# mLSTM with tokens on the partitions, its preparation in the input product, and the later modulation panels in the attention

## The reference

```python
h = rms_norm(x, norm_mix[l])
z = h @ w_in[l]
(m_q, m_k, m_v, m_o, m_i, m_f, a_q, a_k, a_v, i_q, i_k, i_w) = split_cols(z, IN_SIZES)
qk = silu(causal_dwconv(concat([m_q, m_k]), mlstm_conv_w[l], mlstm_conv_b[l]))   # 4 taps
hm = mlstm_chunkwise(q, k, m_v, m_i + i_bias[l], m_f + f_bias[l])                # 4 heads, 64 / 128 wide
hm = sigmoid(m_o) * rms_norm(hm, mlstm_norm[l])
ha = dsa_attention(a_q, a_k, a_v, i_q, rms_norm(i_k, idx_k_norm[l]), i_w * IDX_HEADS ** -0.5, rel_bias)
x = x + concat([hm, ha]) @ w_out[l]
```

## Time and profile before

| | |
|---|---|
| median of 3 runs | 3762.57 us (3760.34 to 3766.36) |
| the profiled execution | 3759.47 us, span 3757.6 us |
| PE busy | 3365.8 us, 90% |
| DVE busy | 1935.9 us, 52% |
| ACT busy | 1489.5 us, 40% |
| POOL busy | 562.7 us, 15% |
| `in1`, until the last gate tile is taken | about 213 us |
| mLSTM stage | 213.6 to 336.9 us |
| index stage and `rel` block | 336.9 to 443.7 us |
| attention stage | 443.7 to 549.2 us |

### The profile page before, as it was taken

The page is one execution under the profiler, slowest core; times in us unless marked ns, Lnnn a source line. Parts: engine busy times, 40 slices in busy tenths (PEclk is TensorE's granted clock), DMA queues, the critical chain, the costliest instruction groups (busy, mean ns, idle before and its releaser), DMA issues. The chain is left out here.

```text
span 3757.6 us, 38218 instructions
## 1 busy us (share of the span) xinstructions
PE 3365.8 (90%) x13472; PEld 2359.3 (63%) x13472; DVE 1935.9 (52%) x2317; ACT 1489.5 (40%) x1918; POOL 562.7 (15%) x304
## 2 busy tenths in 40 slices
PE   7976699999899979597999897799999999999976
PEld 6742465887545558465888544577676777777752
DVE  2046533334424450425003324788888888888835
ACT  3223123443234433113223101566666666565623
POOL 3400002444100024212445100000000000000010
PEclk9966659999999989799999997899999999999988
DMA  3220501222121112121222611899999999999940
GB/s 135 107 90 34 190 1 67 93 108 90 68 83 52 67 45 90 67 90 45 93 108 90 271 67 70 361 398 401 400 401 398 402 404 396 406 395 405 396 191 23
DMA packets 69955, 713.67 MB, mean 190 GB/s; under 512 B 7408, under 2 KB 7792, under 8 KB 29424
## 3 DMA queue, kind: packets, MB, share of 16 engines
q1 hardware_dynamic: 58704, 670.10, 45.1%
q0 software_dynamic: 7056, 25.69, 1.7%
q10 hardware_dynamic: 4112, 16.78, 1.1%
HBM read 672.17 MB, written 40.37 MB: 190 GB/s over the span
## 5 line engine op out<-in xcount | busy, mean ns | idle before, releaser
L136 POOL TENSOR_TENSOR ring_low<-ring,ff_ring_high 128x1024 fp32r<-128x1024 f32 x136 | 331.5, 2471 | 924.0 <-ACT ff_ring_high L131 924.0
L197 PE MATMUL psum<-ff_high,ff_ring_high 128*128 128x512 f32 x832 | 326.0, 392 | 23.2 <-DVE h_low L337 8.6
L199 PE MATMUL psum<-ff_high,ring_low 128*128 128x512 f32 x832 | 325.3, 391 | 0.0
L197 PE MATMUL psum<-ex_high,ex_rows_high 128*128 128x512 f32 x768 | 316.3, 412 | 6.8 <-DVE ring_low L2359 6.8
L199 PE MATMUL psum<-ex_high,ex_rows_low 128*128 128x512 f32 x768 | 301.8, 393 | 0.0
L198 PE MATMUL psum<-h_low,ff_ring_high 128*128 128x512 f32 x704 | 275.1, 391 | 0.0
L2359 DVE TENSOR_TENSOR ex_more_low<-ex_more,ex_high_in_x 128x2048 fp32r<-128x2048 f32 x96 | 219.5, 2286 | 70.4 <-ACT ex_high_in_x L2286 70.4
L2359 DVE TENSOR_TENSOR ring_low<-ring,ex_high 128x2048 fp32r<-128x2048 f32 x96 | 214.3, 2287 | 40.3 <-ACT ex_high L2286 40.3
L1338 PE MATMUL psum<-h,ring 128*128 128x512 f32 x512 | 224.0, 594 | 1.1 <-ACTq L1409 1.1
L2248 PE MATMUL psum<-ex_more,ex_act_t 128*128 128x512 f32 x512 | 224.9, 592 | 0.0
L2286 ACT ACTIVATE ex_high<-ex_more 128x1024 fp32r<-128x1024 f32 x192 | 200.5, 1062 | 57.4 <-PE psum L199 57.4
(11 more groups left out here) (508 smaller groups left out, 6703.7 us busy)
## 6 DMA issues: line engine op xcount, KB each, us to landing
ex_more<-moe_w SPq DMA_DIRECT2D x128, 2048.0 KB, 9.7
ring<-wstream SPq DMA_DIRECT2D x87, 2048.0 KB, 8.1
ring<-moe_w SPq DMA_DIRECT2D x64, 2048.0 KB, 12.0
ex_bias_up<-moe_b SPq DMA_DIRECT2D x32, 1024.0 KB, 8.5
y_rows<-ex_y SPq DMA_DIRECT2D x33, 512.0 KB, 9.2
y_rows<-mx_zero ACTq DMA_DIRECT2D x1, 16384.0 KB, 51.8
ex_bias_down<-moe_b SPq DMA_DIRECT2D x32, 512.0 KB, 8.4
x<-xt SPq DMA_DIRECT2D x8, 256.0 KB, 5.7
```

Of the source, the lines that this page charges most:

```text
L136: e.tensor_tensor(low, full, high.bitcast(F32), ALU.subtract).then_inc(self.low_ready, 1)
L197: pe.matmul(out, a[0], b[0], start=start, stop=False)
L199: return pe.matmul(out, a[1], b[0], start=False, stop=stop)
```

## The change

- **Input product.** The panel with `ik` and the gates comes fourth instead of last. `i`, `f` and `iw` are one tile of 72 rows (i on rows 0 to 3, f from 32, iw from 64) instead of six tiles; `iw` is transposed in the mLSTM stage. The convolution, the Silu of `qk`, the Silu of the modulation's condition and the gates' rows are done in this stage, between the takes (`Rows.act_step`, `Rows.dve_step`, `Rows.convolve`).
- **mLSTM.** Tokens lie on the partitions. The triangular mask is a minimum with 0 or -1e30 before the exponential, on the four diagonal squares alone; the exponential of the rest reads the spread maximum straight from PSUM with the key's value as bias. Numerator and denominator are one product of 129 columns (`mv` has a column of ones, set by POOL). Denominator, floor, norm and root are then 128 x 4 for a head; ACT scales the numerator, PE transposes it, and DVE multiplies by the norm's weight and the gate. Buffers of `prob` and banks alternate by head, and the next head's spread, limits and exponentials are issued ahead.
- **Modulation.** `EARLY = 4`: four products in the mLSTM stage, columns of these in the index stage behind the index scores, the other eight products in the attention at n = 2, 5, ... 23 in bank 7, with their rows copied by ACT, and their 32 columns at n = 32.
- **`rel`** is loaded by SP at the start of the index stage and waited for by DVE at the attention's start; its own block goes. `turn_heads` uses bank 6 alone.

The diff, cut to its core:

```diff
@@ class Modulation
-    EARLY = 3
+    EARLY = 4
@@ class Rows (new)
+    def act_step(self, act, i, tile_ready, dve_took, bank):
+        if i == 7: ... cond = Silu(c2)
+        if i < 4:
+            act.wait_ge(tile_ready, i + 1)
+            act.activation(b1["iq"][:, i, :], bank, ACT.Identity, scale=col("conv_w", 3 * 4 + i),
+                           bias=col("conv_b", i)).then_inc(self.based, 1)
+        if 4 <= i < 8:
+            act.wait_ge(dve_took, i - 3)
+            act.activation(b1["qk"][:, i - 4, :], b1["iq"][:, i - 4, :], ACT.Silu).then_inc(self.qk_ready, 1)
...
+    def convolve(self, dve, i, bank):
+        dve.wait_ge(self.based, i + 1)
+        for tap in (2, 1, 0):
+            back = M_CONV - 1 - tap
...
+            to = b1["iq"][:, i, back:]
+            done = dve.scalar_tensor_tensor(to, bank[:, 0:S - back], col("conv_w", tap * 4 + i), to, ALU.mult, ALU.add)
@@ mlstm_stage, ScalarE
+                def weights(h):
+                    b = h % 2
+                    act.wait_ge(limited, TT * (h + 1))
+                    for j in ORDER:
+                        part = prob[:, b, AT[j]:AT[j] + P]
+                        act.activation(part, part, ACT.Exp).then_inc(weighted, 1)
+                        if j < TT - 1:
+                            act.activation(prob[:, b, AT[j] + P:AT[j] + S - P * j], max_bank[:, P * (j + 1):S], ACT.Exp,
+                                           bias=a_col[:, j, h:h + 1]).then_inc(weighted, 1)
...
+                    if h == 0:
+                        weights(1)
+                        for p in range(2, 4):
+                            act.wait_ge(panel_done, 4 * (p + 1))
+                            mo.take(act, p, psum[:, 4 + p, :]).then_inc(row_ready, 1)
+                    elif h + 1 < MH:
+                        weights(h + 1)
+                    for i in range(TT):
+                        act.wait_ge(nd_done, TT * h + 2 * (i // 2) + 2)
...
+                        act.activation(junk[:, i % 2, :], num(h, i)[:, 0:M_DV], ACT.Square,
+                                       accum_out=squares[:, TT * h + i:TT * h + i + 1]).then_inc(squared, 1)
+                    act.wait_ge(den_ready, 4 * h + 4)
+                    act.activation(den[:, at], den[:, at], ACT.Sqrt).then_inc(std_ready, 1)
+                    act.wait_ge(inverted, h + 1)
...
+                        act.activation(scaled_num[:, q, i, :], num(h, i)[:, 0:M_DV], ACT.Copy,
+                                       scale=inv[:, TT * h + i:TT * h + i + 1]).then_inc(scaled, 1)
@@ mlstm_stage, TensorE
+                for h in range(MH):
+                    if h + 1 < MH:
+                        spread_of(h + 1)
+                    if h == 0:
+                        pe.wait_ge(row_ready, 2)
+                    if h == 1:
+                        pe.wait_ge(row_ready, 4)
+                    if h:
+                        turn(h - 1)
+                    if h >= 2:
+                        pe.wait_ge(mixed, h - 1)
+                    products(h)
+                    if h + 1 < MH:
+                        scores_of(h + 1)
+                    if h == 0:
+                        pe.wait_ge(floor_ready, 1)
+                        for p in range(2, 4):
+                            mo.product(g, pe, p, psum[:, 4 + p, :], panel_done, p + 1)
+                turn(MH - 1)
@@ index_stage
-                for p in range(mo.EARLY, N_ADA):
...
-                    mo.product(g, pe, p, psum[:, p % 4, :], panel_done, done)
+                mo.columns(g, pe, psum[:, 4, :], 0, mo.EARLY).then_inc(columns_ready, 1)
...
-                ring.load_until(sp, FIRST["w_ada"] + N_ADA + SLOTS)
+                sp.dma_start(rel[:, :, :], g.rel_bias).then_inc(rel_in, 16)
@@ attention_stage
+        panel_at = {2 + EVERY * (p - mo.EARLY): p for p in range(mo.EARLY, N_ADA)}     # EVERY = 3
...
+                    if n in panel_at:
+                        done = panel_at[n] - mo.EARLY
+                        if done:
+                            pe.wait_ge(row_ready, done)
+                        mo.product(g, pe, panel_at[n], row_bank, panel_done, done + 1)
+                    if n == NI:
+                        pe.wait_ge(row_ready, N_ADA - mo.EARLY)
+                        mo.columns(g, pe, row_bank, mo.EARLY, N_ADA).then_inc(columns_ready, 1)
...
+                dve.wait_ge(rel_in, 16)
                 soft(0)
```

More of the change, by code:

```diff
@@ L410, in dense_stage @@
                         lambda e, t: e.wait_ge(dve_took, t + 1))
+        if rows is not None:
+            rows.open(sem)
         taken = {"act": [], "dve": []}
@@ L512, in _ @@
                         t.take(dve, psum[:, i % BANKS, :]).then_inc(dve_took, 1)
+                    if rows is not None:
+                        rows.dve_step(dve, i)
                     if sums is not None:
@@ L768, in take, with columns, add_bias @@
         return act.activation(self.part(p), bank, ACT.Copy)
-def mlstm_stage(g, b1, mix, mo):
+    def columns(self, g, pe, bank, first, end):
+        for j in range(4 * first, 4 * end):
+            mm = pe.matmul(bank[:, j:j + 1], self.part(j // 4, j % 4 * P, P), g.ones[:, 0:1], start=True, stop=True)
+        return mm
+    def add_bias(self, g, dve, bank, first, end):
+        at, part = COLS.at["b_ada"], slice(4 * first, 4 * end)
+        return dve.tensor_tensor(g.mod[:, part], bank[:, part], g.cols[:, at + 4 * first:at + 4 * end], ALU.add)
@@ L820, in _ @@
-                for t in range(4):
-                    act.wait_ge(conv_done, t + 1)
-                    act.activation(b1["qk"][:, t, :], conv[:, t, :], ACT.Silu).then_inc(qk_ready, 1)
-                for p in range(mo.EARLY):
+                def weights(h):
[7 more added lines that the diff above has]
+                                           bias=a_col[:, j, h:h + 1]).then_inc(weighted, 1)
@@ L848, in _, with spread_of @@
             @block.tensor
             def _(pe):
-                pe.wait_ge(cond_ready, 2)
-                for p in range(mo.EARLY):
-                    mo.product(g, pe, p, psum[:, 1 + p, :], panel_done, p + 1)
-                pe.wait_ge(rows_ready, 2)
+                def spread_of(h):
+                    if h:
+                        pe.wait_ge(weighted, 7 * h)
+                    pe.matmul(max_bank, g.neg_head[:, h, :], rows.max_row[:, :], start=True, stop=True).then_inc(spread, 1)
@@ new lines, in products, with turn @@
+                def products(h):
+                    for i in range(TT):
+                        pe.wait_ge(prob_ready, 3 * h + min(i, 2) + 1)
+                        for j in range(i + 1):
+                            at = AT[j] + (i - j) * P
+                            mm = pe.matmul(num(h, i), prob[:, h % 2, at:at + P], b1["mv"][:, j, h, :], start=j == 0, stop=j == i)
+                        mm.then_inc(nd_done, 1)
+                def turn(h):
+                    pe.wait_ge(scaled, TT * (h + 1))
+                    for i in range(TT):
+                        mm = pe.transpose(turn_bank(h)[:, i * P:(i + 1) * P], scaled_num[:, h % 2, i, :], g.ident)
+                    mm.then_inc(turned, 1)
@@ new lines, in _ @@
+                spread_of(0)
+                for j in range(TT):
+                    mm = pe.matmul(psum[:, 6, MH * j:MH * j + MH], rows.m_row[:, j * P:(j + 1) * P], g.ident[0:MH, 0:MH],
+                                   start=True, stop=True)
+                mm.then_inc(mcol_psum, 1)
+                for j in range(TT):
+                    mm = pe.matmul(psum[:, 5, IH * j:IH * j + IH], b1["raw"][64:64 + IH, j * P:(j + 1) * P],
+                                   g.ident[64:64 + IH, 64:64 + IH], start=True, stop=True)
@@ L1232, in block_1 @@
             for m in range(4):
-                to = b1[name][:, m, :]
                 e = "act" if m % 2 or name == "o_gate" else "dve"
-                take = copy[e](to) if name != "o_gate" else \
-                    (lambda to: lambda a, bank: a.activation(to, bank, ACT.Sigmoid))(to)
-                tiles.append(Tile([n0 + p], 0 if tokens else m * P, PANEL if tokens else P, h, to, e, take,
-                                  tokens=m if tokens else None, halves=(high, g.h_low)))
-        last = [n0 + 7]
@@ L1265, in block_1 @@
+        mlstm_stage(g, b1, rows, h, mo)
+        with nc.sbuf_tensor("mask", [P, TT, S], F32) as mask, nc.sbuf_tensor("rel", [P, AH, S], F32) as rel:
+            rel_in = g.kept.enter_context(nc.semaphore("rel_in"))
+            index_stage(g, b1, mask, mo, rel, rel_in)
+            attention_stage(g, b1, mask, rel, rel_in, h, mo)
     with ExitStack() as own:
```

415 lines of the change are left out of this document (220 added, 195 removed).

## The result

The changed kernel takes 3645.64 us (median, 3643.75 to 3650.99) against 3761.45 us (3760.01 to 3766.36) for the kernel before in the same comparison: a ratio of 0.9692, interval 0.9675 to 0.9709, or 3.1% faster. The profiled execution has a span of 3641.9 us at a mean granted clock of 0.944 (before: 3757.6 us, 0.926).

What follows compares the result with a forecast made beforehand. TensorE was 90% busy, partly at reduced clock, with limits taken stage by stage: PE, an engine-to-engine chain in mLSTM, DVE in the index stage. Terms -18.1 - 58 - 28.3 + 34.4 = -70 from 3759.5 gave 3690 us, range 3664 to 3714.

Steps and rivals of the forecast that it cites:

- Part 1: Input product: six tiles become one, less a 3.6 us stall waiting for the next panel; -18.1 us.
- Part 3: Index stage: attention starts 0.6 us after the search instead of 28.9, `rel` and early columns hidden; -28.3 us.
- rival D: Attention: panel transfers stand open and products wait for them, slower than before at 3770 us; chance 0.01.
- Part 4: Attention: eight products and 32 columns added, 6 us given back by the clock; +34.4 us, bounds +20 and +43.
- rival A: Attention goes to full clock and stays there, 3648 us; chance 0.10.
- Part 2: mLSTM stage: shorter, overlapping heads of 8.3 to 12 us, length 65 us (bounds 55 and 77); -58 us.
- B: mLSTM and attention: PE-bound at half clock with no gift from the clock, 3707 us; chance 0.22.
- C: mLSTM: DVE or ACT bound by small steps, handoffs costing 26 us more, 3716 us; chance 0.05.

Runs made afterwards that it cites:

- e7_late_burst: Kernel before plus one unused burst of 16 dense matmuls at head 23 of the attention: 3745.12 us, ratio 0.9958.
- e10_mid_burst: Kernel before plus one unused burst of 16 dense matmuls at head 15 of the attention: 3734.74 us, ratio 0.9932.
- e1_burst: Kernel before plus one unused burst of 16 dense matmuls at head 2 of the attention, turn_heads using bank 6 alone: 3762.67 us, ratio 1.0008.
- e2_bursts: Kernel before plus eight unused bursts of 16 dense matmuls, at attention heads 2, 5, ... 23, turn_heads using bank 6 alone: 3743.25 us, ratio 0.9959.
- e11_columns26: Changed kernel with the later columns in one stretch at head 26 instead of behind the last head: 3652.03 us, ratio 0.9716.
- e6_early2: Changed kernel with modulation panels 2 and 3 also moved from the mLSTM into the attention: 3640.54 us, ratio 0.969.
- e8_head0: e4_columns with the eight later products at heads 0, 3, ... 21 instead of 2, 5, ... 23: 3657.73 us, ratio 0.9724.
- e4_columns: Changed kernel with the 32 later columns made panel by panel at heads 4, 7, ... 25 instead of all at head 32: 3637.14 us, ratio 0.9679.
- e9_all: combo with the later products at heads 0, 3, ... 27: 3631.74 us, ratio 0.966.
- combo: Changed kernel with the edits of e6_early2 and e4_columns together: 3635.65 us, ratio 0.9674.

## Why the prediction missed

**The sign and half the steps** held. Part 1 came out at -18.2 for -18.1, with the stall at the place, by the engine and to the time that were worked out. Part 3 came out at -28.4 for -28.3, `rel` and the early columns hidden as costed, and no transfer ever released a product of the attention (rival D's condition).

**Part 4, the give-back of the clock,** is the step that failed. I took 6 us for "where it rises, the next few us of the attention run up to twice as fast" and gave 0.10 to rival A, whose mechanism is what happened for 68 of the stage's 100 us (341.4 to 409.7). Measured against its terms: eight products 17.1 us (one of 3.64, seven of 1.92) where the sum had 27.3 and A had 15.3; the column passes 13.8 us, as the sum had them (13.4), since the clock had fallen by then; all else in the stage 100.4 - 17.1 - 13.8 = 69.5 us for 105.5, so 36 us less where the sum had some 6 and A had 29. Together -5.1 for +34.4. That A's time, 3648, lies so near the measured one is partly luck: its columns were 7 us too cheap and its heads 7 us too dear, and it had the mLSTM 9 us too long and nothing given back. My evidence against A was that 105 us at 96% busy had never risen. That showed that the heads do not raise the clock; e7_late_burst and e10_mid_burst show that the long ones keep it once it is up, two different questions that I took for one. The row that spoke for A, the full clock at a light load from 355 to 360, was weighed too low. The sentence of the Trainium skill, "TensorE: Matmul & The Clock Gate", section "What's actually happening", that I set against the earlier trace rows ("activity releases the throttle") is borne out by the runs of added bursts, as far as dense matmuls go (e1_burst, e7_late_burst, e10_mid_burst; the first burst of e2_bursts raised nothing); the heads' own activity did not release it, and one-column matmuls ended it (e11_columns26).

**Part 2, the length of the mLSTM,** had the right mechanism and too large a size: 65 us taken, 56.8 measured. I took the scores at half clock from the stage before the change, where PE stood between long holes. With fewer holes they ran at 2.42 us from head 1 on, and e6_early2 shows that this needs no panels 2 and 3. That the stage ended at 251.9, where full clock throughout had been worked out to end at 251, is partly luck, since the clock was 0.80 in the mean and the products of heads 1 and 2 ran largely at half. Head 0 waited for modulation row 3 as listed, and the head periods of 9.0 to 6.5 us begin within 8.3 to 12 and end below, the last ones having no next head's weights on ScalarE.

**Rivals.** B and C would have been slower than the forecast and did not show (ScalarE waited 0.25 us for VectorE's reciprocal, and 0.82 more for its small steps only in the last head, where no table load covered them). The misses, 39.5 us in part 4 and 8.8 in part 2, with 0.2 from parts 1 and 3, make 48.5, of which 2.8 were given back behind block 1. That an untouched stage can differ by 2.6 us between two executions was in no term. Three slips of the working are small beside this: the 9.2 us ahead of the attention are 9.5 in the earlier trace rows, 3690 is the profiled execution's figure, the median's would have been 3693, and the three upper bounds add up to -46 and not -48.

**The range** was closed at 3664, with A left out as part of the 0.17. A whole stage whose clock is in doubt was worth 40 us on one side only, and belonged inside it.

## What to carry to other kernels

Where a stage is TensorE-bound at clock 0.50, ask two things separately: what would raise the clock, and whether the work behind would keep it. One burst of 16 dense matmuls ahead of the long heads, 3.6 us of pure waste, made the kernel before 25 us faster (3734.7 us); the same burst ahead of the short ones won nothing. Real dense work that has to go somewhere belongs in a place behind which the heavier steps follow. A long run of one-column matmuls cost less in small pieces between other work (8.4 us for 13.8), but look at the clock behind the pieces. Where a result depends on the clock among short steps, time more than one placement (e8_head0 and e4_columns differ by 20 us for two heads of shift, e9_all and combo by 4 the other way), and put both clocks into the range.

## What was not expected of the hardware

- A TensorE stage at 96% busy stood at half clock for 105 us; its heads 16 to 31, the same work, ran at full clock at 93% busy, depending only on one burst of 3.6 us ahead of them (e10_mid_burst).
- The same burst at the same head raised the clock in e1_burst and did not in e2_bursts. In e1_burst the clock fell again among short heads, with no PE wait above 0.63 us since the burst.
- 64 one-column matmuls with their weight loads, without a hole, brought the clock down from 1.00 to 0.50 within 2 us of their start and took 12.7 us; in pieces of eight they took 1.05 us each and left it up behind seven of eight pieces in e4_columns, but behind none in e8_head0.
- In a stretch 1160 us behind block 1, which the change does not touch, the same two matmuls took 1.10 us in one execution and 2.04 in another. Thirteen of fourteen traces show the shorter time; what decides it stays open.
- Why eight products at heads 2 to 23 hold the clock among heads of 128 keys and at heads 0 to 21 do not stays open. What the traces show is where the second product falls against the clock's fall (343.95, with no fall near it; 341.03, with the fall at 341.2); what sets the time of that fall, and what part the pieces of columns have in it, was not isolated.
